# Attention on one core: the probabilities of heads 0 to 3 turned by VectorE and a DRAM scratch

## The reference, cut to what matters

```python
q, k, v = jnp.split(h @ w_qkv, 3, axis=-1)
q = rope(rms_norm(q.reshape(B, S, A_HEADS, A_HEAD_DIM), q_gain), pos)
k = rope(rms_norm(k.reshape(B, S, A_HEADS, A_HEAD_DIM), k_gain), pos)
...
s_own = jnp.where(kpos[None, :] <= qpos[:, None], s_own, NEG)
...
p = jax.nn.softmax(jnp.concatenate(scores, axis=-1), axis=-1).astype(v.dtype)
out = jnp.einsum('bhqk,bhkd->bhqd', p_parts[0], v_own)
```

## Time and profile before

| what | value |
|---|---|
| median of 3 runs | 662.67 us (662.6 to 663.25) |
| the profiled execution's own time | 662.9 us |
| its span | 661.1 us |
| PE busy | 655.7 us, 99% of the span |
| PEld busy | 553.4 us, 84% |
| DVE busy | 430.3 us, 65% |
| ACT busy | 332.4 us, 50% |
| POOL busy | 26.8 us, 4% |
| granted clock of PE | 1.0 (full) throughout |
| mean rate of the DMA engines | 196 GB/s |

### The profile page before, as it was taken

One profiled execution on the slowest core, in us unless ns is written; L12 is line 12 of the kernel. 1 busy time (PEld: TensorE's weight loads), 2 busy tenths in 40 slices (PEclk: granted clock), 3 DMA queues, 4 the chain that ended last, 5 costly groups with the idle time before them and its releaser, 6 DMA issues.

```text
span 661.1 us, 8673 instructions
## 1 busy us (share of the span) xinstructions
PE 655.7 (99%) x3248; PEld 553.4 (84%) x3248; DVE 430.3 (65%) x481; ACT 332.4 (50%) x435; POOL 26.8 (4%) x29
## 2 busy tenths in 40 slices
PE   8999999999999999999999999999999999999998
PEld 7888888888888888888888888888888888888887
DVE  6798656877776445549984765765588777744531
ACT  7777664655554333454445555554465555533320
POOL 0163000000000000000000000000000000000000
PEclk9999999999999999999999999999999999999999
DMA  9965457766555657554655657649847655565500
GB/s 325 389 220 190 128 152 246 202 188 188 187 189 192 192 192 257 194 183 154 225 192 193 191 161 276 197 149 288 234 148 216 193 193 183 191 208 195 187 1 32
DMA packets 90766, 129.30 MB, mean 196 GB/s; under 512 B 3312, under 2 KB 50928, under 8 KB 90736
## 3 DMA queue, kind: packets, MB, share of 16 engines
q1 hardware_dynamic: 90448, 127.58, 59.6%
q0 software_dynamic: 288, 1.31, 0.5%
HBM read 124.68 MB, written 4.19 MB: 195 GB/s over the span
## 4 chain that ended last, share of the span: by engine, by line
PE 99%; DVE 0%; issue 0%; DVEq 0%
PE acc L635 23%; PE acc L539 19%; PE acc L541 19%; PE acc L540 19%; PE acc L638 11%; PE acc L586 1%; PE acc L583 1%; PE acc L592 1%; PE acc L658 1%; PE scr L541 1%; PE scr L540 1%; PE scr L539 1%; PE scr L671 1%; PE scr L682 1%; PE scr L703 1%; PE scr L766 1%
## 5 line engine op out<-in xcount | busy, mean ns | idle before, releaser
L1046 DVE TENSOR_TENSOR lo<-raw,hi 128x2048 fp32r<-128x2048 f32 x108 | 247.1, 2288 | 109.6 <-ACT hi L806 109.5
L806 ACT ACTIVATE hi<-raw 128x2048 fp32r<-128x2048 f32 x108 | 207.0, 1918 | 139.4 <-PE acc L541 137.4
L635 PE MATMUL acc<-h_both,hi 128*128 128x512 f32 x640 | 224.0, 396 | 0.0
L638 PE MATMUL acc<-h_both,lo 128*128 128x256 f32 x640 | 178.3, 279 | 0.0
L635 PEld LDWEIGHTS acc<-h_both,hi 128*128 128x128 f32 x640 | 120.1, 188 | 28.5
L638 PEld LDWEIGHTS acc<-h_both,lo 128*128 128x128 f32 x640 | 120.5, 188 | 0.0
L539 PE MATMUL acc<-hi,aT_hi 128*128 128x512 f32 x252 | 98.1, 389 | 0.0
L541 PE MATMUL acc<-hi,aT_lo 128*128 128x512 f32 x252 | 98.0, 389 | 0.0
L540 PE MATMUL acc<-lo,aT_hi 128*128 128x512 f32 x252 | 98.0, 389 | 0.0
L539 PE MATMUL acc<-hi,h_both 128*128 128x512 f32 x208 | 83.4, 401 | 0.0
L541 PE MATMUL acc<-hi,h_both 128*128 128x512 f32 x208 | 81.2, 390 | 0.0
(11 more groups left out here) (132 smaller groups left out, 582.5 us busy)
## 6 DMA issues: line engine op xcount, KB each, us to landing
raw<-in_mlp_w SPq DMA_DIRECT2D x64, 1024.0 KB, 5.4
raw<-in_r_w_in SPq DMA_DIRECT2D x24, 1024.0 KB, 5.1
raw<-in_a_w_qkv SPq DMA_DIRECT2D x8, 1024.0 KB, 9.8
raw<-in_r_w_out SPq DMA_DIRECT2D x8, 1024.0 KB, 5.2
raw<-in_a_w_qkv SPq DMA_DIRECT2D x16, 256.0 KB, 6.1
raw<-in_a_w_o SPq DMA_DIRECT2D x4, 1024.0 KB, 5.0
z_rows<-stage_a SPq DMA_DIRECT2D x32, 64.0 KB, 1.8
stage_b<-z_rows SPq DMA_DIRECT2D x8, 256.0 KB, 2.8
```

Source lines behind the costliest of these rows:

```text
L635: nc.tensor.matmul(bank, feat_view(hi, s)[:, kt, o * P:(o + 1) * P], h_both[:, kt, :, :].rearrange("p b t -> p (b t)"), start=kt == 0, sto ...
L638: m = nc.tensor.matmul(bank[:, 0:SEQ], feat_view(lo, s)[:, kt, o * P:(o + 1) * P], hT_hi[:, kt, :], start=False, stop=kt == KD - 1)
L806: nc.scalar.activation(hi[:, s, :], raw[:, s, :], ACT.Copy).then_inc(hi_ready, 1)
L1046: nc.vector.tensor_tensor(lo[:, s, :], raw[:, s, :], hi[:, s, :].bitcast(F32), ALU.subtract).then_inc(lo_ready, 1)
```

## The change

Heads 0 to 3 no longer use PE for turning their probabilities. After the normalisation DVE turns each 32 x 32 block of the head (one instruction of 128 x 384) into p_blocks; SP writes these in four transfers of 48 KB to a DRAM scratch, which puts the blocks in place, and reads the head back in one transfer of 192 KB into pT. The product with v reads pT in runs of 32 columns. ACT's copy for these heads goes too. SP does this in its own order: write head s, load chunk 12+s, read head s. From half step 16 to 19 a third order, middle, holds, with "left" and "var" first. The low part of chunk 9 moves from half step 14 to 15, that of chunk 10 from 15 to 17. The diff, with the context lines that matter:

```diff
@@ -128,9 +128,10 @@
     at[SCALES_AT].append(("scales", 0))
     first = ["T", "square", "var", "rope", "factors", "low", "raw", "high", "left"]
     early = ["scales", "rope", "high", "low", "N", "v", "raw", "left", "var", "T", "A", "P", "S", "E"]
+    middle = ["left", "var", "rope", "high", "low", "N", "v", "raw", "T", "A", "P", "S", "E"]
     late = ["N", "A", "S", "v", "high", "O", "P", "E", "low"]
     for k in range(SLOTS):
-        first_to_last = first if k < EARLY else early if k < LATE else late
+        first_to_last = first if k < EARLY else early if k < MIDDLE else middle if k < LATE else late
         at[k].sort(key=lambda what: (first_to_last.index(what[0]), VAR_ORDER.index(what[1]) if what[0] == "var"
                                      else what[1]))
 
@@ -149,8 +150,9 @@
 O_AT = A_AT
 V_AT = [19, 20, 23, 23]
 HIGH_AT = {4: 6, 6: 7}
-LOW_AT = {1: 3, 3: 4, 5: 7, 7: 9, 9: 11, 11: 13, 13: 14, 17: 18}
+LOW_AT = {1: 3, 3: 4, 5: 7, 7: 9, 9: 11, 11: 13, 13: 15, 15: 17, 17: 18}
 EARLY = 10
+MIDDLE = 16
 LATE = 20
 SCHEDULE = attention_schedule()
 SQUARES_BEFORE = sum(what == "raw" for k in range(SQUARE_AT) for what, _ in SCHEDULE[k])
@@ -179,6 +181,7 @@
 def program(nc, x_in, tables, a_w_qkv, a_w_o, r_w_in, r_w_out, mlp_w1, mlp_w2,
             out):
     x_rows = nc.dram_tensor("x_rows", (2, TT, P, 4, P), F32, kind="Internal").ap()
+    p_rows = nc.dram_tensor("p_rows", (4, P, 4, 3 * 32), F32, kind="Internal").ap()
     z_rows = nc.dram_tensor("z_rows", (HR, TT, P, 4, P), F32, kind="Internal").ap()
     rope_a, rope_r, decay, causal, gcol_src, ident_src, xT_src = tables
     with ExitStack() as ctx:
@@ -240,6 +243,7 @@
         rope_t = rope_in[:, 0:4 * P].rearrange("p (t a d) -> p t a d", t=TT, d=P)
         gains = rope_in[:, 4 * P:6 * P].rearrange("p (i d) -> p i d", d=P)
         rope_g = at("rope_g", 55 * KB, [P, 2, TT, 2, P])
+        p_blocks = at("p_blocks", 61 * KB, [P, 2, 384])
         mask = at("mask", 59 * KB, [P, 384])
 
         zT_hi = at("zT_hi", 0, [P, 16, SEQ], F32R)
@@ -302,6 +306,9 @@
         p_ready = sem("p_ready")
         pTp_ready = sem("pTp_ready")
         pT_ready = sem("pT_ready")
+        p_blocks_ready = sem("p_blocks_ready")
+        p_out = [sem(f"p_out{h}") for h in range(4)]
+        p_in = [sem(f"p_in{h}") for h in range(4)]
         o_ready = sem("o_ready")
         oT_hi_ready = sem("oT_hi_ready")
         oT_ready = sem("oT_ready")
@@ -422,8 +429,22 @@
             sp.dma_start(gcol[:], gcol_src).then_inc(gcol_in, 16)
             for c in range(7, 12):
                 load_qkv(c)
+
+            def write_probs(h):
+                sp.wait_ge(p_blocks_ready, h + 1)
+                for i in range(4):
+                    rows = p_rows[h].rearrange("(j r) i c -> i r j c", j=4)[i]
+                    sp.dma_start(rows, p_blocks[32 * i:32 * i + 32, h % 2, :].rearrange("p (j c) -> p j c", j=4)
+                                 ).then_inc(p_out[h], 16)
+
+            def read_probs(h):
+                sp.wait_ge(p_out[h], 64)
+                sp.dma_start(pT[:, h, :], p_rows[h].rearrange("d i c -> d (i c)")).then_inc(p_in[h], 16)
+
             for s, (n, kg) in enumerate(WO_ORDER):
+                write_probs(s)
                 load(C_WO // 4, s, tok_view, wo_w[n, kg])
+                read_probs(s)
             load_w1(0)
             load_w2(0)
             with sp.Fori(0, 2) as i:
@@ -684,8 +705,8 @@
 
             def transpose_p(h):
                 pe.wait_ge(p_ready, h + 1)
-                if h >= 1:
-                    pe.wait_ge(pT_ready, h)
+                if h >= 5:
+                    pe.wait_ge(pT_ready, h - 4)
                 b = scr[:, 1, :]
                 p = probs[:, h % 3, :]
                 nc.tensor.transpose(b[:, 0:P], p[:, 0:P], ident[:])
@@ -694,16 +715,22 @@
 
             def attend(h):
                 pe.wait_ge(v_ready, 2 + 2 * (h // 4))
-                pe.wait_ge(pT_ready, h + 1)
+                if h < 4:
+                    pe.wait_ge(p_in[h], 16)
+                    p = pT[:, h, :].rearrange("p (i b c) -> p b i c", i=4, b=3)
+                    first, second = p[:, 0:2], p[:, 2]
+                else:
+                    pe.wait_ge(pT_ready, h - 3)
+                    first, second = pT[:, h % 4, 0:SEQ], pT[:, h % 4, SEQ:384]
                 if h == 1:
                     pe.wait_ge(qkT_ready, 8)
                 if h >= 2:
                     pe.wait_ge(oT_ready, h - 1)
                 bank = scr[:, BANK_O[h % 2], :]
-                nc.tensor.matmul(bank[:, 0:SEQ], v_att[:, 0, h * P:(h + 1) * P], pT[:, h % 4, 0:SEQ],
+                nc.tensor.matmul(bank[:, 0:SEQ], v_att[:, 0, h * P:(h + 1) * P], first,
                                  start=True, stop=False)
-                nc.tensor.matmul(bank[:, P:SEQ], v_att[:, 1, h * P:(h + 1) * P],
-                                 pT[:, h % 4, SEQ:384], start=False, stop=True).then_inc(o_ready, 1)
+                nc.tensor.matmul(bank[:, P:SEQ], v_att[:, 1, h * P:(h + 1) * P], second,
+                                 start=False, stop=True).then_inc(o_ready, 1)
 
             def behind(k):
                 for what, i in SCHEDULE[k]:
@@ -711,7 +738,7 @@
                         transpose_rot(i)
                     elif what == "S":
                         scores(i)
-                    elif what == "P":
+                    elif what == "P" and i >= 4:
                         transpose_p(i)
                     elif what == "A":
                         attend(i)
@@ -896,9 +923,8 @@
                                          ).then_inc(e_ready, 1)
 
             def store_pT(h):
-                act.wait_ge(pTp_ready, h + 1)
-                if h >= 4:
-                    act.wait_ge(o_ready, h - 3)
+                act.wait_ge(pTp_ready, h - 3)
+                act.wait_ge(o_ready, h - 3)
                 nc.scalar.copy(pT[:, h % 4, :], scr[:, 1, 0:384]).then_inc(pT_ready, 1)
 
             def head_hi(h):
@@ -1177,8 +1203,10 @@
                 if h == 0:
                     dve.wait_ge(mask_in, 16)
                 dve.wait_ge(pow_ready, POWER_NO[4 * (h // 4) + 1])
-                if h >= 3:
-                    dve.wait_ge(pTp_ready, h - 2)
+                if 3 <= h < 7:
+                    dve.wait_ge(p_blocks_ready, h - 2)
+                elif h == 7:
+                    dve.wait_ge(pTp_ready, 1)
                 mx = small[:, 40 + 2 * (h % 4):42 + 2 * (h % 4)]
                 for t, (a, b) in enumerate(((0, P), (P, 384))):
                     dv.mark(nc.vector.tensor_tensor_reduce(
@@ -1197,6 +1225,13 @@
                     i = nc.vector.tensor_scalar(probs[:, h % 3, a:b], probs[:, h % 3, a:b],
                                                 rs[:, t:t + 1], None, ALU.mult)
                 i.then_inc(p_ready, 1)
+                if h < 4:
+                    dve.wait_ge(p_ready, h + 1)
+                    if h >= 2:
+                        dve.wait_ge(p_out[h - 2], 64)
+                    nc.vector.transpose(p_blocks[:, h % 2, :].rearrange("p (j b c) -> p b j c", j=4, b=3),
+                                        probs[:, h % 3, :].rearrange("p (b j c) -> p b j c", b=3, j=4)
+                                        ).then_inc(p_blocks_ready, 1)
 
             def head_lo(h):
                 dve.wait_ge(oT_hi_ready, h + 1)
```

## The result

The changed kernel takes **664.23 us** (median of 15 runs; 662.67 to 665.53) against 662.6 for the kernel before in the same measurement: a ratio of 1.0025, 95% interval 1.0015 to 1.0035, so +1.65 us by the ratio (the medians are 1.63 apart). A second measurement gave 1.0026 (1.0015 to 1.0038). It is slower, by a quarter of a per cent; the forecast was 663.6, or +0.9, with a range to 665.0, so the sign and the range held and the size was short by 0.7.

The account below looks back on a forecast made before the run. The prediction took PE as the bound (99% of the chain): 1.6 us of removed transposes, against stalls of 0.7 at block 5 and 1.8 at block 7, gave +0.9, so 663.6 us, range 661.3 to 665.0.

Parts of the forecast that it names:

- The block transpose at 0.56, delay 0.6: On DVE, each head's new transpose takes 0.56 us and delays what follows by 0.6 us.
- Stall at block 5: PE's transposes of block 5 wait about 0.7 us for ACT's copy of block 4 into qkT.
- DVE from half step 14 to 17: DVE's order there: rope 6 at 53.3, rope 7 unmoved, var 7 again at about 62.5 us.
- Stall at block 7: PE's transposes of block 7 wait 1.8 us, until about 69.15, for ACT's copy of block 6 into qkT.
- The first stall doesn't add to this: Whatever PE gains or loses before the transposes of block 7, it goes on at 69.15 us.
- The port pair: POOL may hold the last small instruction of DVE's masking up to 0.3 us more, making the end 0.3 later.
- Transfers: Writes and reads of heads 0 to 3 land in time; head 3, the tightest, by 76 to 78, margin 3 us or more.
- The strided product: Product with v reading pT in runs of 32 columns: taken as no cost, from above 2.6 us.
- Downstream everything hangs on PE and has time to spare, so the 0.9 stays: Behind the transposes of block 7, nothing changes the +0.9 us up to the run's end.
- The gain coming through: Rival: copy of block 6 ready by 67.3 despite later masking; time 661.1 to 661.8 us, chance 0.17.
- The dearer product: Rival: runs of 32 columns slow PE's product with v, 666.2 us at double; chance 0.26 together with a longer half-step-17 chain.
- the late read: Rival: the read for head 3's product with v lands late, from 3 us of lateness; 664 to 666 us, chance 0.03.

Follow-up runs that it names:

- e2: Changed kernel with the masking of head 3 ahead of chunk 10's low part and block transposes at the end of their half step; ratio 0.9985 against before.
- e5: Changed kernel with only the block transposes on DVE moved to the end of their half step; ratio 1.0015 against the kernel before.
- e1: Changed kernel with one order entry moved: masking of head 3 ahead of the low part of chunk 10; ratio 0.9984 against the kernel before.
- e8: Changed kernel with ACT's copy of block 6 into qkT ahead of the high part of chunk 12; ratio 1.0011 against the kernel before.
- e4: Changed kernel with the old lists: block transposes kept, low parts of chunks 9 and 10 and the order put back; ratio 1.0024 against before.
- e11: The version of e2 run again unchanged, for a second ratio; 0.9980 against the kernel before.

## Why the prediction was right, point by point

- **PE bound, so every wait counts: right.** The stretch lengthened by 0.92 us, where the sum said 0.9. But the waits in brackets are not what PE lost: -1.6 + 0.84 + 1.94 would be +1.2. The starts of PE's matmuls give what was lost:

| PE, from start to start | before | after | difference |
|---|---|---|---|
| block 4 to the next weight matmul | 0.68 | 0.35 | -0.33 |
| on to block 5 | 2.85 | 3.46 | +0.61 |
| block 5 to the scores of head 2 | 0.77 | 0.47 | -0.30 |
| on to the scores of head 3 | 6.60 | 6.15 | -0.45 |
| on to block 6 | 3.43 | 3.40 | -0.03 |
| on to block 7 | 3.21 | 4.92 | +1.71 |
| block 7 to the next weight matmul | 0.69 | 0.39 | -0.30 |
| on to the first transposes of x | 39.48 | 39.49 | +0.01 |

- **The terms of the sum: each a little too large.** About 1.4 us were freed (not 1.6), and 0.6 and 1.7 us were lost at blocks 5 and 7 (the sum had 0.7 and 1.8). That -1.4 + 0.6 + 1.7 is again +0.9 is partly luck. "P" of head 2 was taken at 0.6 from the weight loads, idle time and all; from start to start it was 0.45. And before, the weight load of block 5 started 0.23 us ahead of its matmul (53.87 and 54.10), but behind a wait only 0.03 (54.13 and 54.16), so the idle time in brackets is 0.2 us more than what PE loses. e2, in which no time is lost, has 1.43 us less.
- **The block transpose at 0.56, delay 0.6: right.** It took 0.58; the next instruction started 0.50 after it (49.62), and its own wait ahead of it cost about 0.1.
- **Stall at block 5, 0.7: 0.84 of idle weight loads, 0.61 on the matmuls.** Place and releaser right; e5 and e2 remove it by moving one instruction.
- **DVE from half step 14 to 17: right.** Rope 6 at 53.14 (said 53.3), rope 7's last step 1.46 us under POOL's scaling, var 7 at 62.31 (said 62.5), the low part at 62.45, the masking at 64.65 (said 64.8).
- **Stall at block 7, 1.8, until 69.15: 1.94 of idle weight loads, 1.71 on the matmuls, until 69.07.** e1 shows that the masking behind the low part is its cause. By e8, POOL is next at 68.6, inside the range I gave it (66.6 to 68.9).
- **"The first stall doesn't add to this": half right.** The waits don't add, as the text says, but what makes the first one moves the chain behind the second too: 0.55 us by e5. The working carried that 0.6 into N 1 and rope 6, where it ate what the moved low part had freed, but never said that the second stall contains it.
- **The port pair.** The Trainium skill's rule (SBUF — State Buffer, section "SBUF: two separate sides") would have held the masking's last small instruction by up to 0.3 us. It took 0.16 at 65.32 and was not held, though POOL's power was on record until 65.60 (62.62 + 2.98). The kernel before shows the same: POOL's power ran from 63.48 to 64.49, and neither the masking's last instruction nor the low part behind it took longer for it:

```profile
63.98 0.16 DVE L1189 SCALAR_TENSOR_TENSOR small<-small 128x2 f32<-128x2 f32 x1
64.06 2.28 DVE L1046 TENSOR_TENSOR lo<-raw,hi 128x2048 fp32r<-128x2048 f32 x1
```

```profile
63.48 1.01 POOL L491 TENSOR_TENSOR small<-head_sums,half 128x4 f32<-128x4 f32 x1
```

Against POOL's multiplication the traces agree with the rule: in e4 the masking's last instruction took 0.57 us at 64.59, until the multiplication ended at 65.14; in the changed kernel the normalisation of head 3 took 1.13 us (67.79) instead of 0.55, beside the multiplication up to 68.58. The other way round the power was held: 2.98 us instead of 1.01, behind the start of the low part of chunk 10.

- **Transfers: right.** The read of head 3 was issued at 72.54, and the longest of the four took 5.0 us, so it was there by 77.5; A 3 loads at 80.91. The pieces of 384 B did not slow the writes in a way that matters: 1.7 us for 48 KB. The Trainium skill's line on pieces under 512 B (DMA: Bandwidth & Descriptors, section "Specifications") changes nothing here; no run compared the two sizes.
- **The strided product costs nothing: right.** From A 0 to the scores behind it: 72.32 to 72.97 after, the 0.65 us of before.

```profile
72.32 0.59 PE L730 MATMUL scr<-pT,v_att 128*128 128x256 f32 x2
...
72.97 0.39 PE L701 MATMUL scr<-qkT 128*128 128x128 f32 x2
```

- **The step that was too small: "Downstream everything hangs on PE and has time to spare, so the 0.9 stays."** Nothing downstream waits anew, and the three later stages show no cost that belongs to the change. But the measured +1.65 (at least +1.0 by the interval) is more than the stretch. Three profiles of each put 0.3 us of it into the start of block 4, ahead of the first place where PE's work was changed (the rest is the mix of paces that the timed runs drew, or what three profiles do not show). Over all thirteen profiles that start lies between 49.62 and 50.45, and e11, with the changed kernel's work on PE up to there, starts it at 49.74, so chance alone could make the 0.3. But eight of the nine ratios in the table are 0.1 to 0.8 us further to the slow side than their stretch (only e1 is 0.2 the other way), so a small cost outside the stretch is not excluded. This was not settled.
- **The chances.** 664.23 lies above the 664.0 up to which the prediction saw its forecast (chance 0.54); it is the outcome "slower by over 0.2%", to which it gave 0.27. The mechanism is the one forecast, but the time came out higher than its 0.9 us account for.
- **The rivals.** The gain coming through needed 1.8 us less on the chain, and e1 gave just this at block 7, with the first stall left (stretch -0.87). The dearer product and the late read did not occur.

## What to carry to other kernels

When PE is the bound and a job is taken from it, follow the chain that feeds PE's next small job before counting the gain: here 1.4 us were freed and 2.3 us lost, 1.7 of them because one 2.2 us instruction stood ahead of a 0.8 us one that another engine waited for. Take gains and losses from the starts of the matmuls; the idle time in brackets before a weight load was 0.2 us more than PE lost, at block 5, at block 7 and in e2. Within a half step, put what another engine waits for ahead of what nobody needs soon; that one entry was worth 1.8 us. And compare a stretch between two marks of the trace when the whole time scatters more than the effect.

## What the runs showed that I had not expected

The same stage ran in either of two durations with the granted clock at 1.0 throughout: 88.83 or 90.5 us for the first half of an MLP, in the same kernel from one execution to the next. These draws are worth up to 4.3 us over three stages, more than the whole effect of this change. With them taken off, the three profiled executions of the kernel before lie within 0.7 us of each other instead of 2.0. What sets the pace was not tried.
